# A decoder layer on one core: attention probabilities turned by transposes, and the forget-gate sums spread once per head

## What is computed

```python
c = jnp.cumsum(log_f, axis=1)                      # FoX, per head
s = jnp.einsum('bhqd,bhkd->bhqk', qi, kt) * scale
s = s + ci[..., None] - c[:, :, None, :]           # the c of the query cancels in the softmax
s = jnp.where(k_pos[None, :] <= q_pos[:, None], s, -jnp.inf)
p = jax.nn.softmax(s, axis=-1)
o = jnp.einsum('bhqk,bhkd->bhqd', p, vt)

s = jnp.einsum('bshd,bnhd->bhsn', q, k) * (MEM_HEAD_DIM ** -0.5)   # memory attention, 4 heads of 256
p = jax.nn.softmax(s, axis=-1)
o = jnp.einsum('bhsn,bnhd->bshd', p, v).reshape(B, S, D_MODEL)
```

## Time and profile before

| | |
|---|---|
| median of 3 runs | 1317.06 us |
| the three runs | 1316.52, 1317.06, 1320.66 us |
| span of the profiled execution | 1321.0 us |
| its own time | not listed apart from the three runs; the span is 3.9 above the median |
| TensorE busy | 1264.8 us (96%) |
| VectorE, ScalarE, GpSimd busy | 409.3, 443.8, 497.3 us (31, 34, 38%) |
| mean granted TensorE clock | 0.971 |

### The profile page before, as it was taken

How to read it: one execution, slowest core, us unless ns; L and a number is a source line. 1 busy time by engine, 2 the same in 40 slices (tenths; PEclk the granted TensorE clock), 3 DMA queues, 4 the chain that set the end, 5 groups by cost and what they waited for, 6 DMA issues and landing times.

```text
span 1321.0 us, 15790 instructions
## 1 busy us (share of the span) xinstructions
PE 1264.8 (96%) x5795; PEld 1027.1 (78%) x5795; DVE 409.3 (31%) x675; ACT 443.8 (34%) x681; POOL 497.3 (38%) x240
## 2 busy tenths in 40 slices
PE   7999999999998989999999899989899999999997
PEld 5788888888876767777767777768688888888886
DVE  4422323210017443533431523431731313130004
ACT  3423233231134443343423444433442323231113
POOL 4344444444442341211105474204244444444442
PEclk9999999999998989999879899999899999999999
DMA  5233333222221221111202343102133333322211
GB/s 179 65 96 95 95 95 96 99 97 96 96 90 58 68 74 39 36 45 41 72 16 80 97 144 112 48 31 91 54 96 96 95 95 95 95 96 96 95 64 64
DMA packets 83320, 108.77 MB, mean 82 GB/s; under 512 B 8686, under 2 KB 53836, under 8 KB 83276
## 3 DMA queue, kind: packets, MB, share of 16 engines
q1 hardware_dynamic: 83120, 108.14, 25.2%
q10 hardware_dynamic: 156, 0.04, 0.0%
HBM read 106.06 MB, written 2.10 MB: 82 GB/s over the span
## 4 chain that ended last, share of the span: by engine, by line
PE 41%; issue 39%; POOL 13%; DVE 4%; ACT 2%; POOLq 0%; DVEq 0%; ACTq 0%
POOL w_lo L550 13%; PE bank L1374 13%; PE bank L1375 13%; PE bank L1376 13%; PE bank L1392 1%; PE bank L1382 1%; DVE acc L957 1%; PE bank L1616 1%; PE bank L1399 0%; DVE acc L954 0%; DVE qm_lo L1142 0%; ACT w_hi L614 0%; DVE h L1014 0%; DVE f_fin L1359 0%; DVE tmp L1134 0%
## 5 line engine op out<-in xcount | busy, mean ns | idle before, releaser
L550 POOL TENSOR_TENSOR w_lo<-raw,w_hi 128x1024 fp32r<-128x1024 f32 x176 | 429.4, 2440 | 768.3 <-ACT w_hi L614 768.3
L1374 PE MATMUL bank<-xh,w_hi 128*128 128x512 f32 x992 | 394.6, 398 | 17.8 <-DVE xl L943 15.6
L1375 PE MATMUL bank<-xl,w_hi 128*128 128x512 f32 x992 | 389.5, 393 | 0.0
L1376 PE MATMUL bank<-xh,w_lo 128*128 128x512 f32 x992 | 389.5, 393 | 0.0
L614 ACT ACTIVATE w_hi<-raw 128x1024 fp32r<-128x1024 f32 x176 | 186.4, 1059 | 514.5 <-PE bank L1376 510.3
L1374 PEld LDWEIGHTS bank<-xh,w_hi 128*128 128x128 f32 x992 | 188.3, 190 | 62.4 <-issue 16.6
L1376 PEld LDWEIGHTS bank<-xh,w_lo 128*128 128x128 f32 x992 | 188.1, 190 | 40.4
L1375 PEld LDWEIGHTS bank<-xl,w_hi 128*128 128x128 f32 x992 | 188.4, 190 | 37.5
L1374 PE MATMUL bank<-mid_hi,w_hi 128*128 (+1 forms) x352 | 138.5, 393 | 0.0
L1375 PE MATMUL bank<-mid_lo,w_hi 128*128 (+1 forms) x352 | 137.6, 391 | 0.0
L1376 PE MATMUL bank<-mid_hi,w_lo 128*128 (+1 forms) x352 | 137.3, 390 | 0.0
(11 more groups left out here) (227 smaller groups left out, 1357.3 us busy)
## 6 DMA issues: line engine op xcount, KB each, us to landing
raw<-in_ffn_w_gu SPq DMA_DIRECT2D x176, 256.0 KB, 2.9
raw<-in_ffn_w_down SPq DMA_DIRECT2D x88, 256.0 KB, 2.7
raw<-in_mix_w_in SPq DMA_DIRECT2D x48, 256.0 KB, 2.8
raw<-in_mem_w_kv SPq DMA_DIRECT2D x32, 256.0 KB, 3.3
raw<-in_mix_w_out SPq DMA_DIRECT2D x16, 256.0 KB, 3.0
raw<-in_mem_w_q SPq DMA_DIRECT2D x16, 256.0 KB, 3.0
raw<-in_mem_w_o SPq DMA_DIRECT2D x16, 256.0 KB, 2.8
x_tok<-in_x SPq DMA_DIRECT2D x4, 512.0 KB, 5.3
```

The source lines that it names most:

```text
L550: gp.tensor_tensor(w_lo[:, n % SPLIT, :], raw[:, n % RAW, :], w_hi[:, n % SPLIT, :].bitcast(F32), ALU.subtract).then_inc(lo_ready, 1)
L1374: pe.matmul(dst, w[0], x[0], start=start, stop=False, skip_group_check=loose)
L1375: pe.matmul(dst, w[0], x[1], start=False, stop=False, skip_group_check=loose)
L1376: return pe.matmul(dst, w[1], x[0], start=False, stop=stop, skip_group_check=loose)
```

## The change

For the memory units: the exponential still goes to `prob`, which has three buffers now; VectorE multiplies `prob` in place by the reciprocal over all w columns, and TensorE turns each 128-key block with a transpose against the identity.

For the FoX units the same, and besides: the cumulative sums of a head are spread over 128 partitions once, by one matmul of 512 columns with all 128 rows (`cum_rows`), into a bank of the scores' rotation; it is issued just ahead of the scores of the previous head's last block. ScalarE copies that bank to `cum_b`, two buffers (`cum_spread`). VectorE's maximum becomes one `tensor_tensor_reduce`: -(scores + cum_b) into `prob`, with the minimum of it as accumulator. The exponential works in place with scale -1. The mask product comes first and is 256 columns wide, a zero block beside the diagonal block (in front of it, or for i = 0 behind it), so the first block's scores are 256 columns wide too. The last value product of a head is widened from 128 to 256 columns over a block of zeros, set once by VectorE. `cum_hl` is filled in the lower half of the partitions only, and `sel32` needs two selects instead of four.

The diff, cut to its core:

```diff
-        prob = sb("prob", [P, 2, SEQ], at=shared + 80 * kib)
-        norm_diag = sb("norm_diag", [P, 2, P], at=shared + 84 * kib)
+        prob = sb("prob", [P, PROBS, SEQ], at=shared + 80 * kib)
...
-            for base in (0, -32, -64, -96):
+            for base in (0, -32):
...
+                def cum_spread(hd):
+                    act.wait_ge(cb_done, hd + 1)
+                    if hd >= 2:
+                        act.wait_ge(maxed, TC * (hd - 1))
+                    act.activation(cum_b[:, hd % 2, :], bank[cum_slot(hd) % 2][:, :], ACT.Copy).then_inc(cb_ready, 1)
+                if phase == FOX:
+                    cum_spread(0)
                 for k in range(len(units) + late + 2):
+                    if phase == FOX and k < len(units) - 1 and k % TC == TC - 1:
+                        cum_spread(k // TC + 1)
...
-                        if u >= 2:
-                            act.wait_ge(pturned, u - 1)
-                        act.activation(prob[:, u % 2, 0:w], s_bank(phase, k)[:, 0:w], ACT.Exp, ...)
+                        if mem:
+                            act.wait_ge(pturned, u - PROBS + 1)
+                            act.activation(prob[:, u % PROBS, 0:w], s_bank(phase, k)[:, 0:w], ACT.Exp,
+                                           bias=nmx[:, r], accum_out=rs[:, r]).then_inc(expd, 1)
+                        else:
+                            act.activation(prob[:, u % PROBS, 0:w], prob[:, u % PROBS, 0:w], ACT.Exp,
+                                           bias=nmx[:, r], scale=-1.0, accum_out=rs[:, r]).then_inc(expd, 1)
...
+                            if i == 0:
+                                dve.wait_ge(cb_ready, hd + 1)
+                            if u >= PROBS:
+                                dve.wait_ge(pturned, u - PROBS + 1)
+                            dve.tensor_tensor_reduce(prob[:, u % PROBS, 0:w], s_bank(phase, k)[:, 0:w],
+                                                     cum_b[:, hd % 2, 0:w], -1.0, -NEG, ALU.add, ALU.min,
+                                                     accum_out=nmx[:, r]).then_inc(maxed, 1)
...
-                        if u >= 2:
-                            dve.wait_ge(pturned, u - 1)
-                        dve.tensor_scalar(norm_diag[:, u % 2, :], ident[:, :], rr[:, r], None,
+                        dve.tensor_scalar(prob[:, u % PROBS, 0:w], prob[:, u % PROBS, 0:w], rr[:, r], None,
                                           ALU.mult).then_inc(normed, 1)
...
+                def cum_rows(hd):
+                    fox_free(cum_slot(hd))
+                    pe.matmul(bank[cum_slot(hd) % 2][:, :], sel[:, hd, :], cum_hl[:, :],
+                              start=True, stop=True).then_inc(cb_done, 1)
...
-                        three(dst, (q_hi[r, c, tok], q_lo[r, c, tok]), (k_hi[r, c, 0:w], k_lo[r, c, 0:w]),
-                              True, False)
-                        pe.matmul(dst[:, w - P:w], ident_r[:, :], causal[:, :], start=False, stop=False,
+                        part = slice(0, 2) if i else slice(1, 3)
+                        pe.matmul(dst[:, w - 2 * P:w], ident_r[:, :],
+                                  causal[:, part, :].rearrange("p j n -> p (j n)"), start=True, stop=False,
                                   skip_group_check=True)
-                        last = pe.matmul(dst, sel[r, hd, :], cum_hl[r, 0:w], start=False, stop=True)
+                        last = three(dst, (q_hi[r, c, tok], q_lo[r, c, tok]), (k_hi[r, c, 0:w], k_lo[r, c, 0:w]),
+                                     False, True, True)
...
-                        last = pe.matmul(p_bank(phase, k)[:, j * P:(j + 1) * P], prob[:, u % 2, j * P:(j + 1) * P],
-                                         norm_diag[:, u % 2, :], start=True, stop=True)
+                        last = pe.transpose(p_bank(phase, k)[:, j * P:(j + 1) * P],
+                                            prob[:, u % PROBS, j * P:(j + 1) * P], ident[:, :])
...
-                        q0 = 0 if mem else j * P
+                        q0 = 0 if mem else min(j, 2) * P
```

More of the change, by code:

```diff
@@ L118 @@
 N_FOX = len(FOX_UNITS)
+PROBS = 3
 FOX, MEM_A, MEM_B = range(3)
@@ L1293, in mixer @@
                 gates()
-                dve.wait_ge(cum_hi, 2)
-                for r in (32, 96):
-                    dve.tensor_tensor(cum_hl[r:r + FOX_H, :], cum[:, :], cum_hl[0:FOX_H, :].bitcast(F32),
-                                      ALU.subtract).then_inc(cum_lo, 1)
+                dve.wait_ge(cum_hi, 1)
+                dve.tensor_tensor(cum_hl[32:32 + FOX_H, :], cum[:, :], cum_hl[0:FOX_H, :].bitcast(F32),
+                                  ALU.subtract).then_inc(cum_lo, 1)
                 in_evacuate(1)
                 in_evacuate(2, (0, 1))
+                for t in (pt_hi, pt_lo):
+                    dve.memset(t[:, TC - 1, 2 * P:3 * P].bitcast(F32), 0.0).then_inc(pt_zero, 1)
                 attention(FOX)
@@ L1582, in scores @@
                     w = key_width(mem, i)
-                    if k in s_free:
+                    if phase == FOX:
+                        if i == TC - 1 and hd + 1 < FOX_H:
+                            cum_rows(hd + 1)
+                        fox_free(fox_slot(k))
+                        w = max(w, 2 * P)
+                    elif k in s_free:
                         pe.wait_ge(*s_free[k])
@@ L1625, in output @@
                     pe.wait_ge(pt_l, u0 + done + 1)
+                    if phase == FOX and hd == 0:
+                        pe.wait_ge(pt_zero, 2)
                     if (hd, e) in o_free:
@@ L1636, in output @@
                     last.then_inc(pv_done, 1)
+                if phase == FOX:
+                    cum_rows(0)
                 for k in range(len(units) + late + 1):
```

46 lines of the change are left out of this document (30 added, 16 removed).

## The result

The changed kernel takes 1300.36 us (median of four runs, 1298.83 to 1304.36) against 1316.79 us (1315.96 to 1320.66): ratio 0.9869, 95% interval 0.9846 to 0.9893, 16.4 us less. The forecast was 1297.0 us, 20 us less. The profiled execution has a span of 1299.2 us and a time of 1300.92 us; against the span of 1321.0 before, that is 21.8 us less. So 16.4 us is what the change saved, and the 21.8 is only for finding out where.

What follows compares the result with a forecast made beforehand. The prediction took TensorE's own stream to bound the FoX attention. Scores 12.8, turn 8.6, waits -4.6 and memory attention 3.5 sum to 20.3, rounded 20 us saved: 1297 us, range 1291 to 1304.

Steps and rivals of the forecast that it cites:

- the scores: FoX score products on TensorE: fewer changes between 64 and 128 rows save 14.6 us, row products add 1.8; net 12.8.
- the turn: FoX turning of probabilities: one transpose record a block instead of two, 0.107 us less for 80 blocks, 8.6 us.
- Waits: TensorE's added waits in the FoX attention, at three places: 4.6 us (2 to 9).
- at the start: Start of the FoX phase: first add waits for ScalarE's copy, v_lo pair behind it; +1.0 us (0.3 to 1.5).
- Iterations 24 and 28: FoX turns held because GpSimd's w_lo delays VectorE's scale: 1.35 instead of 0.43 us each, +1.8 us.
- Iterations 11 to 13: FoX iterations where VectorE evacuates a filled group and multiplies decays: TensorE waits away its gain, about 1.8 us.
- Memory attention: Memory stage saving 3.5 us: filled half 1.7, second half's dependent chain 1.1, third probability buffer 0.7.
- rival D: Slower through the clock: the grant drops inside the FoX stretch; about 110 us lost over the whole stretch, 1407; chance 0.04.
- A: VectorE becomes what ends last, with a 1.12 us add and more held scales: saving 13, 1304 us; chance 0.17.
- C: A transpose of the probabilities takes as long as the two records did: saving 8 to 9, 1308.5 us; chance 0.02.
- B: No waits come, the third buffer opens the memory chain, or a half-clock stretch ends sooner: saving 26, 1291; chance 0.09.
- the forecast case: Whole kernel: the main expectation, a saving of 17 to 24 us; chance 0.68.

Runs made afterwards that it cites:

- turn_only: Kernel before with only the turn changed in both attention stages: probabilities scaled in place, three buffers, transposes; 1303.58 us against 1318.32, ratio 0.988.
- scores_only: Changed kernel with the old turn (two buffers, product with the diagonal block), keeping mask first and bias from VectorE; 1310.12 us, ratio 0.9936.
- mask_first: Kernel before with only the mask product moved ahead of the three 64-row products, still 128 wide; 1303.39 us, ratio 0.9914.
- mask_turn: Kernel before with the mask first (128 wide) and the turn by transposes, bias still a 64-row product in every unit; 1297.83 us, ratio 0.9864.
- after_again: The changed kernel profiled and timed once more, unchanged; 1299.39 us against 1315.41, ratio 0.9878.
- early_spread: Changed kernel with the first head's row product one token block earlier and its ScalarE copy ahead of the first v_hi evacuations; 1299.07 us, ratio 0.9857.
- late_round: Changed kernel with the rounding of a weight block one iteration later at iterations 15, 23 and 27; 1296.18 us, ratio 0.9826.
- scale_first: Changed kernel with VectorE's reciprocal and scale of the unit before ahead of this unit's add in the FoX stage; 1299.15 us, ratio 0.9878.
- best: scale_first plus early_spread's edits, first exponential ahead of the v_hi pair, v_lo pair behind the second add; 1295.3 us, ratio 0.9862.
- best2: Changed kernel with the edits of early_spread and late_round, and the start's rounding behind the first two exponentials; 1291.68 us, ratio 0.9812.
- best3: mask_turn with the same three late roundings and later start rounding as best2; 1296.33 us, ratio 0.9849.

## Why the prediction was right

The stages side by side; busy and waits are PE's in the stretches and the wait lists:

| kernel | stage, us | busy | waits | clock |
|---|---|---|---|---|
| before | 147.8 | 146.5 | 1.3 | 1.00 |
| turn_only | 139.8 | 137.2 | 2.6 | 1.00 |
| scores_only | 139.1 | 134.9 | 4.2 | 1.00 |
| mask_first | 138.5 | 135.5 | 3.1 | 1.00 |
| mask_turn | 131.1 | 125.9 | 5.3 | 1.00 |
| after | 135.1 | 128.8 | 6.4 | 0.97 |
| after_again | 135.1 | 128.7 | 6.4 | 0.97 |
| early_spread | 130.7 | 125.4 | 5.4 | 1.00 |
| late_round | 128.7 | 125.0 | 3.7 | 1.00 |
| scale_first | 133.6 | 126.8 | 6.9 | 0.99 |
| best | 132.7 | 125.7 | 7.1 | 1.00 |
| best2 | 126.5 | 124.9 | 1.7 | 1.00 |
| best3 | 126.8 | 125.2 | 1.7 | 1.00 |

(The stages of early_spread, best and best2 from their first mask product; the 0.35 us that best2's row has ahead of that are taken off its busy time.)

**Stream of the FoX attention.** Forecast 12.8 for the scores and 8.6 for the turn, 21.4. Measured: 21.1 from before to after at full clock, 21.5 to late_round. Apart, the turn gave 9.3 and the scores 11.6, within an us of their terms. The unit costs were right to 0.01 us in the 512-wide unit. What the sum didn't separate is where the gain comes from: of the 11.6 us measured for the scores, the mask's place alone gives 11.0.

**Waits.** Forecast +4.6, measured +5.1 by PE's list (+7.2 by the weight load's, on which the forecast stood), but not all where I put them. By distances from start to start: at the start +1.0 (0.3 to 1.5) forecast; TensorE waits 2.0 there, where the kernel before waits 0.6 for its first turn, so +1.4. The queue was the right one; the waiter was not. I had the first add and the v_lo pair waiting, and overlooked that the mask product of iteration 1 needs the row product's bank. Iterations 24 and 28: 1.35 us each forecast, 1.3 each measured, for 0.4 each before, and late_round shows the cause. Iteration 16, 0.6 us, was missed: I had put it among the ten splits with two quarters or a value product as cover, but its turn has one quarter ahead of it too. Iterations 11 to 13: 1.8 forecast, 2.2 less 0.6 measured.

**Memory attention.** Forecast 3.5, measured 0.8 (63.2 to 62.5 us). The rows of the two kernels, and of early_spread:

```profile
818.40:881.70 63.30, 54.78 (x301) 46.25 (x302) 29.13 (x81) 23.76 (x63) 9.61 (x4) 0.97 0.12 42
```

```profile
798.90:861.40 62.50, 53.01 (x269) 42.71 (x270) 30.03 (x81) 23.99 (x63) 9.58 (x4) 0.95 0.12 43
```

```profile
795.10:855.90 60.80, 52.55 (x269) 42.93 (x270) 29.65 (x81) 24.09 (x63) 9.61 (x4) 0.94 0.13 44
```

The timelines of PE divide the stage at its value products (us, from start to start):

| part | before | after | early_spread |
|---|---|---|---|
| to the value products at the end of the filled half | 35.4 | 33.9 | 33.9 |
| those products, and on to the next turn | 7.9 | 8.7 | 8.6 |
| the chain of the second half, to its last value products | 17.3 | 15.7 | 15.7 |
| the last value products | 2.6 | 4.2 | 2.6 |

The filled half gained 1.5 us, where 1.7 was forecast, and the chain 1.7, where 1.8 was: the turn, the scale and the third buffer did what the sum said, and turn_only, which has only these, has the same four lengths as the kernel after. What took the gain away is again the clock. After, half-clock stretches of 3.4 us lie on the first value products (833.6 us) and on the last (857.5), and before, a single one in the chain (863.1). The last twelve products take 4.2 us instead of 2.6 by it. In early_spread the second stretch falls into the chain, where it costs nothing visible (scale_first has no second stretch and the same 15.7), and the stage is 1.7 us shorter at a lower mean clock. Of the nine kernels with the new turn five have the late stretch and take 62.5 us, and four don't and take 60.8 to 60.9; the three with the old turn take 63.2 to 63.4. So the gain is 2.4 us without the late stretch and 0.8 with it. This term is what the forecast had most wrong: not the chain, but a clock term that it put at nothing. Whether the 0.8 us of the second part belong to the clock alone isn't shown, since all kernels with the new turn have the stretch there, and what the stretch in the chain cost before isn't either.

**The clock.** I had given the sum no term for it in either stage, and as rival D only the whole 20 us. By one of my own signs the prediction is wrong here: the clock row of the FoX stretch was not to fall below 1.00, and it is 0.97. The 3.4 us are a sixth of what D asks for, and they don't come by its mechanism: that the transposes as such don't lower the clock is shown by turn_only and mask_turn at 1.00, and the stretch follows a wait. With it the account closes on the profiles: 21.1 less 5.1 less 3.4 makes 12.6 of the stage's 12.8. The Trainium skill, "TensorE: Matmul & The Clock Gate", Part 4, says that the full clock doesn't engage for transposes; for up to four at a time amid ordinary matmuls those same rows don't agree.

**Rivals.** A falls: the add costs 0.69 us and VectorE is busy for 63 of 135 us. C falls with turn_only. B's 1291 us is what best2 reaches, once the waits are taken away by hand. The total came out inside the range with luck. On the profiles, losses of 6 us that weren't foreseen (2.7 in the memory attention, 3.4 by the clock in the FoX stage) met some 7 us that the change didn't earn (4.8 behind the FoX attention, 2.3 ahead of it). On the medians the saving of 16.4 us is below the forecast case, and inside the range only because that reached up to 1304 us for rival A, whose mechanism didn't occur.

## What to carry to other kernels

Before pricing new arithmetic on another engine, price the order: moving one full-height product out of the middle of half-height ones gave 11 us of TensorE's time, and the bias that went to VectorE with it gave nothing in the stage. When work is moved to a queue, ask for each result who else uses its bank, and look at the queue's neighbours at the start of the phase: the longest single wait was there. Before a missing gain is put down to the chain, cut the stage into parts and look at the clock in each: here the chain gave what was forecast, and a half-clock stretch on the full products behind it took 1.6 us.

## What the runs showed of the hardware that was not expected

- A VectorE scale with both operands in SBUF and a pointer that meets a GpSimd subtraction ends 0.1 to 0.3 us after that subtraction, having started 0.5 to 1.2 us into it: 1.93 us in place of 0.29 at 128 columns, 1.46 and 1.67 in place of 0.49 at 512. The add from PSUM and SBUF and the pt_lo subtraction from PSUM beside the same subtraction aren't held.
- The last short product ahead of a change from 128 to 64 rows pays as well: four turn records take 0.54 us ahead of a 64-row product and 0.36 ahead of the 128-row mask.
- A wait of 2.0 us in an otherwise full stream can be followed by 6.8 us at the lower clock level, 5.4 us together; in the profiles at hand that went with a shift of half a microsecond in the start, and the cause isn't shown.
- Half-clock stretches elsewhere move with any edit: the same gated linear attention took between 27.4 and 34.1 us, with stretches of 10.2 to 23.9 us at the lower level in and behind it. What such a stretch costs depends on where it falls: 3.4 us of it cost 1.6 us on full value products of the memory attention and nothing visible in the chain ahead of them. A difference of a few us between two profiles is therefore not a saving until the stage is named.
